# Gated scan: near levels as compact strips of 32 keys, far levels as exact products, factor products on one engine

## Chip, cores and metric

The kernel runs on one core of a Trainium2 chip. The time is that of the device for one execution, in microseconds, as the median of three runs. The core has TensorE (matrix products, into PSUM), VectorE, ScalarE and GpSimd (elementwise work), SyncE (here the weight DMAs) and 16 DMA engines. Each engine runs a program of its own, and they meet at semaphores.

## What is computed

The reference is two transformer-like blocks on 512 tokens of width 1024. The part that matters here is the first block's gated scan, once forward and once backward, for 4 heads with 128 key channels:

```python
def step(state, inp):
    qc, kc, vc, gc = inp
    bcum = jnp.cumsum(gc, axis=1)
    total = bcum[:, -1]
    new_state = jnp.exp(total)[..., None] * state + jnp.einsum(
        'bshk,bshv->bhkv', kc * jnp.exp(total[:, None] - bcum), vc)
    decay = jnp.exp(jnp.where(causal, bcum[:, :, None] - bcum[:, None], -jnp.inf))
    scores = jnp.einsum('bthk,btshk,bshk->bhts', qc, decay, kc)
    o = jnp.einsum('bhts,bshv->bthv', scores, vc) + jnp.einsum(
        'bthk,bhkv->bthv', qc * jnp.exp(bcum), state)
    return new_state, o

o_lf, _ = chunk_gated_scan(ql, klf, il, llf, s_cf, True)
o_lb, _ = chunk_gated_scan(flip(ql), flip(klb), flip(il), flip(llb), s_cb, True)
hg = hgrn2_readout(o_lf + flip(o_lb), p[..., O_HG:O_FN], hg_norm_g[l])
```

The score of query t and key s carries, for each channel, the product of all gates between them. Queries later than the key belong to the forward scan, earlier ones to the backward scan.

## The kernel before

Everything is fp32 with channels on the 128 partitions and tokens along the free axis. The scan works on blocks of 128 tokens (`TT` = 4 blocks of the 512 tokens, `TAT` = 6 with the context). `hq` holds the queries (one 512-column row for each of `HH` = 4 heads), `kk` the keys of both directions (d = 0 forward, 1 backward; 768 columns a head, context included), `ff` the gates, `q_dec` the queries with factors, kept in `hT`.

Instead of a cumulated exponent the kernel builds the products of gates by doubling. Level `lev` of `LEVELS` = 7 deals with the pairs of key and query that lie in the two halves of one group of 2 x 2^lev tokens. A unit is one level of one head: `lev_units` has 28, level by level with the four heads inside, unit u writing PSUM bank u % 4. For each unit:

- TensorE (L1143, L1144) multiplies, for each block of 128 tokens, all 128 keys of the block with the 64 queries of the later halves (forward), then with the 64 queries of the earlier halves (backward). So 8 products, most of whose entries belong to no pair of this level.
- VectorE multiplies the queries of the halves by the factors (L1099, L1101), picks the entries of this level out of the bank into the score matrix `wsc` with the constant mask `cross{lev}` (L1103), and halves the table of factors of the unit before (`shrink`, L1081).
- GpSimd multiplies the keys of the halves by the factors (L1066, L1068).

The entries of a token with itself come first: TensorE multiplies the sum of both directions' keys with the queries, 4 products a head (L1127), and ScalarE copies the bank to `wsc` (L1116), which shares the memory of `hq` and so waits for the products of the queries with the gates (L1073 on VectorE, L1055 on GpSimd).

Between the units TensorE's program computes modulation vectors: 64 `mod_step`s (L456), each a 128x32 stationary with 512 moving columns into one of four strips of 32 partitions, 2 or 3 after each unit, with a weight chunk of 2 MB for each eight. After each eighth, ScalarE copies the row (L466), and `mod_turn` (L472, 4 products with 2 columns) turns it. The first step of a chunk waits for the copy of the row before. The weights come through a ring of three slots by SyncE's queue. A barrier ends the block; the next one (L1207, L1231, L1216 to L1219) forms the states and the output out of `wsc`.

The order within each engine is the order in which the program is written. TensorE's unit u waits for the queries, the keys and the selection of unit u - 4, the same head's unit of the level before; VectorE's and GpSimd's units wait for TensorE's unit (`lev_done`) and for the factors of u - 4 (`t_upd`).

Of the kernel before, what the change touches and what calls it, by code (L numbers as in the profile page):

```python
# [19 lines left out]
U32 = mybir.dt.uint32  # L20
ALU = mybir.AluOpType
# [60 lines left out]
def constants():  # L82
# [18 lines left out]
    for lev in range(LEVELS):  # L101
        out[f"cross{lev}"] = level_mask(lev, True) + level_mask(lev, False)
# [91 lines left out]
def program(nc, weights, consts_d, vecs_d, x_d, ctx_d, out_d):  # L194
    ctx = ExitStack()
    with ctx:
# [29 lines left out]
        def bank(b, n=512):  # L226
            return psum[:, b * 512:b * 512 + n]
# [12 lines left out]
        ARENA = 22760  # L240
# [725 lines left out]
        o_hg = sb("o_hg", [P, 2, T], s6)  # L966
        k_sum = state.rearrange("p a b c -> p (a b c)")[:, 0:HH * T].rearrange("p (h n) -> p h n", h=HH)
# [73 lines left out]
        def products_of(ap, lev):  # L1041
# [8 lines left out]
            sem(n) for n in ("diag_done", "w_set", "qf_set", "qb_set", "lev_done", "sel_done", "q_upd", "k_upd", "t_upd"))  # L1050
        with nc.Block() as block:
            @block.gpsimd
            def _(pool):
                for h in range(HH):
                    pool.tensor_tensor(q_dec[1][:, h, :], hq[:, h, :], ff[:, 1, h, 0:T], ALU.mult).then_inc(qb_set, 1)  # L1055
                for u in range(NU):
                    lev, h = lev_units[u]
                    pool.wait_ge(lev_done, u + 1)
                    if lev >= 1:
                        pool.wait_ge(t_upd, u - 3)  # L1060
                        pool.wait_ge(k_upd, u - 3)
                    for d in range(2):
                        k1, k2 = halves(kk[:, d, h, :], lev)
                        _, _, (t1, t2) = products_of(ff[:, d, h, :], lev)
                        if d == 0:
                            pool.tensor_tensor(k1, k1, t2, ALU.mult)  # L1066
                        else:
                            pool.tensor_tensor(k2, k2, t1, ALU.mult).then_inc(k_upd, 1)  # L1068

            @block.vector  # L1070
            def _(dve):
                for h in range(HH):
                    dve.tensor_tensor(q_dec[0][:, h, :], hq[:, h, :], ff[:, 0, h, 0:T], ALU.mult).then_inc(qf_set, 1)  # L1073

# [9 lines left out]
                for u in range(NU):  # L1084
# [6 lines left out]
                    else:  # L1091
                        dve.wait_ge(t_upd, u - 3)
                        dve.wait_ge(q_upd, u - 3)
                        dve.wait_ge(sel_done, u - 3)
                    for d in range(2):
                        q1, q2 = halves(q_dec[d][:, h, :], lev)
                        _, _, (t1, t2) = products_of(ff[:, d, h, 0:T], lev)
                        if d == 0:
                            dve.tensor_tensor(q2, q2, t1, ALU.mult)  # L1099
                        else:  # L1100
                            dve.tensor_tensor(q1, q1, t2, ALU.mult).then_inc(q_upd, 1)  # L1101
                    mask = C(f"cross{lev}").bitcast(U32).rearrange("p (o n) -> p o n", o=1).to_broadcast([P, TT, P])
                    dve.copy_predicated(wsc[:, h, :].rearrange("p (i n) -> p i n", i=TT), mask,  # L1103
                                        bank(u % 4).rearrange("p (i n) -> p i n", i=TT)).then_inc(sel_done, 1)
# [5 lines left out]
            @block.scalar  # L1110
            def _(act):
                for h in range(HH):
                    act.wait_ge(diag_done, h + 1)
                    act.wait_ge(qf_set, h + 1)
                    act.wait_ge(qb_set, h + 1)
                    act.copy(wsc[:, h, :], bank(4 + h % 2)).then_inc(w_set, 1)  # L1116
                for ch in range(4, 12):
                    mod_copy(act, ch)

            @block.tensor  # L1120
            def _(pe):
                for h in range(HH):
# [1609 lines left out]
```

## Time and profile before

| | us |
|---|---|
| median of 3 runs | 2749.49 |
| lowest, highest | 2744.36, 2750.85 |
| the profiled execution | 2755.42 |
| its span | 2753.3 |
| TensorE, VectorE, ScalarE, GpSimd busy in the span | 2437.4, 1002.5, 734.5, 198.6 |
| the block with the levels | from 424.6 to 531.3 |

Busy time is the time in which at least one instruction of the engine runs. Matmuls overlap each other in the array, so the mean duration of one (some 270 ns with 64 columns) is much longer than the distance between two; the distance between starts is what counts. In the records each fp32 matmul stands as two matmuls with a weight load each. The granted clock is 1.00 for TensorE's upper level of 2.4 GHz and 0.50 for 1.2 GHz.

### The profile page before, as it was taken

What the parts mean: (1) busy time and instruction counts of PE and PEld (TensorE: products, weight loads), DVE (VectorE), ACT (ScalarE), POOL (GpSimd) and SP (SyncE); (2) the same over time, 40 slices, a digit from 0 to 9 for tenths busy, and PEclk for the clock granted to TensorE, in tenths of its full rate; (3) what the DMA queues carried; (4) which work ended last, traced back from release to release, by engine and by line L of the source; (5) the groups of instructions that cost most, each with busy time, mean ns of one, the idle gap of its engine ahead of it and who ended that gap; (6) DMA issues with size and microseconds to landing.
All of it is one profiled execution on the core that took longest, in us unless ns stands there. A gap on an engine that the chain in (4) does not pass through costs nothing. (4 is left out here: it accounts for less than half of the span.)

```text
span 2753.3 us, 32259 instructions
## 1 busy us (share of the span) xinstructions
PE 2437.4 (89%) x13690; PEld 1839.1 (67%) x13690; DVE 1002.5 (36%) x1585; ACT 734.5 (27%) x1271; POOL 198.6 (7%) x239
## 2 busy tenths in 40 slices
PE   6979999987999988996687999998986777799997
PEld 3533456775888866886665888886864555588885
DVE  2013118533333334635124333423225543343333
ACT  2122200023222222313212322322213552332331
POOL 0000006400000000012000000000022440000000
PEclk8988999888999997997558999998997998899999
DMA  6120013311223111200011222212210003122210
GB/s 281 38 90 17 21 41 131 145 46 47 105 79 122 69 70 62 92 31 2 4 62 62 92 92 92 92 64 92 92 33 1 1 1 123 61 92 94 110 72 31
DMA packets 16110, 196.33 MB, mean 71 GB/s; under 512 B 1888, under 2 KB 3040, under 8 KB 3936
## 3 DMA queue, kind: packets, MB, share of 16 engines
q1 hardware_dynamic: 15392, 190.72, 18.5%
q10 hardware_dynamic: 576, 3.56, 0.3%
q8 instruction: 109, 1.79, 0.3%
q14 instruction: 33, 0.27, 0.0%
HBM read 190.08 MB, written 2.10 MB: 70 GB/s over the span
## 5 line engine op out<-in xcount | busy, mean ns | idle before, releaser
L1503 DVE TENSOR_TENSOR wsp_mlp<-ring,wsp_mlp 128x1024 fp32r<-128x1024 f32 x128 | 156.7, 1225 | 447.8 <-ACT wsp_mlp L1474 447.8
L1474 ACT CAST wsp_mlp<-ring 128x1024 fp32r<-128x1024 f32 x128 | 133.9, 1048 | 491.4 <-PE psum L1459 489.4
L1456 PE MATMUL psum<-hs_mlp,wsp_mlp 128*128 128x512 f32 x512 | 201.7, 394 | 36.2 <-DVE wsp_mlp L1503 36.2
L1456 PE MATMUL psum<-acts_mlp,wsp_mlp 128*128 128x512 f32 x512 | 202.4, 395 | 0.0
L1458 PE MATMUL psum<-hs_mlp,wsp_mlp 128*128 128x512 f32 x512 | 201.3, 393 | 0.0
L1459 PE MATMUL psum<-hs_mlp,wsp_mlp 128*128 128x512 f32 x512 | 201.1, 393 | 0.0
L1459 PE MATMUL psum<-acts_mlp,wsp_mlp 128*128 128x512 f32 x512 | 199.3, 389 | 0.0
L1458 PE MATMUL psum<-acts_mlp,wsp_mlp 128*128 128x512 f32 x512 | 199.2, 389 | 0.0
L1503 DVE TENSOR_TENSOR wsp_ffn<-ring,wsp_ffn 128x1024 fp32r<-128x1024 f32 x66 | 80.8, 1225 | 246.2 <-ACT wsp_ffn L1474 246.2
L414 PE MATMUL psum<-hsev,wspev 128*128 128x512 f32 x672 | 156.6, 395 | 0.4 <-DVE arena_low L1647 0.3
L1456 PE MATMUL psum<-hs_ffn,wsp_ffn 128*128 128x512 f32 x352 | 138.1, 392 | 19.5 <-DVE wsp_ffn L1503 19.5
L414 PEld LDWEIGHTS psum<-hsev,wspev 128*128 128x128 f32 x672 | 127.8, 191 | 28.4 <-DVE arena_low L1647 1.6
L1474 ACT CAST wsp_ffn<-ring 128x1024 fp32r<-128x1024 f32 x66 | 69.1, 1048 | 266.2 <-PE psum L1459 265.2
L1458 PE MATMUL psum<-hs_ffn,wsp_ffn 128*128 128x512 f32 x352 | 137.7, 391 | 0.0
L1459 PE MATMUL psum<-hs_ffn,wsp_ffn 128*128 128x512 f32 x352 | 137.6, 391 | 0.0
L1456 PEld LDWEIGHTS psum<-hs_mlp,wsp_mlp 128*128 128x128 f32 x512 | 97.5, 190 | 58.3 <-DVE wsp_mlp L1503 37.9
L349 PE MATMUL psum<-hT,ring 128*128 128x512 f32 x288 | 125.3, 592 | 0.9 <-PEq L862 0.9
L1458 PEld LDWEIGHTS psum<-hs_mlp,wsp_mlp 128*128 128x128 f32 x512 | 97.4, 190 | 20.5
L1459 PEld LDWEIGHTS psum<-hs_mlp,wsp_mlp 128*128 128x128 f32 x512 | 97.4, 190 | 20.3
L1456 PEld LDWEIGHTS psum<-acts_mlp,wsp_mlp 128*128 128x128 f32 x512 | 96.1, 188 | 21.7 <-issue 1.9
L1458 PEld LDWEIGHTS psum<-acts_mlp,wsp_mlp 128*128 128x128 f32 x512 | 96.1, 188 | 21.6 <-issue 1.9
L1459 PEld LDWEIGHTS psum<-acts_mlp,wsp_mlp 128*128 128x128 f32 x512 | 96.1, 188 | 19.8
(391 smaller groups left out, 4152.9 us busy)
## 6 DMA issues: line engine op xcount, KB each, us to landing
ring<-weights SPq DMA_DIRECT2D x85, 2048.0 KB, 7.9
ring<-weights SPq DMA_DIRECT2D x3, 1024.0 KB, 5.7
cst<-consts ACTq DMA_DIRECT2D x1, 2209.0 KB, 14.3
xT<-xin SPq DMA_DIRECT2D x2, 1024.0 KB, 7.2
out<-xT SPq DMA_DIRECT2D x1, 2048.0 KB, 6.3
ring<-weights SPq DMA_DIRECT2D x1, 1280.0 KB, 5.9
mixT<-ctxin ACTq DMA_DIRECT2D x1, 1024.0 KB, 15.5
ring<-weights SPq DMA_DIRECT2D x2, 512.0 KB, 3.4
```

What stands on the lines that cost most here:

```text
L349: last = pe.matmul(out, lhs(k), rhs(k), start=(k == 0), stop=(k == n - 1))
L414: last = pe.matmul(out, wsp[:, q % 2, a, i * 512 + j * P:i * 512 + (j + 1) * P], hs[:, b, 2 * u + i, :], **ends)
L1456: pe.matmul(tile_bank(g, j), w_hi, src[:, 0, k0 + i, :], start=(first and i == 0), stop=False)
L1458: pe.matmul(tile_bank(g, j), w_hi, src[:, 1, k0 + i, :], start=False, stop=False)
L1459: last = pe.matmul(tile_bank(g, j), w_lo, src[:, 0, k0 + i, :], start=False, stop=(last_k and i == 1))
L1474: act.copy(wsp[:, q % 2, 0, :], raw_view(q)).then_inc(s["w_hi"], 1)
L1503: dve.tensor_tensor(wsp[:, q % 2, 1, :], raw_view(q), wsp[:, q % 2, 0, :].bitcast(F32), ALU.subtract).then_inc(s["w_lo"], 1)
```

## The change

Levels 0 to 4 (`NEAR`) concern only pairs within 32 tokens. For them each block of 128 keys is taken as four strips of 32: a product takes 32 keys and the 16 queries of their halves, and writes a strip of 32 partitions. The four strips lie side by side on partitions, 32 columns for each block, so a bank's first 128 columns hold a unit, and the selection (mask `pair{lev}`) goes into a compact `w_near` of 128 columns a head. Levels 5 and 6 (`far`) compute only the entries that belong to the level, each in its place of the bank; before level 5, `nearest` places `w_near` on the diagonal of the bank by products with parts of the identity. Banks 0 to 3 then hold the full score matrices, and ScalarE copies them to `wsc` at the end. The products of the keys with the factors move from GpSimd into VectorE's program (`keys`), with the starting products of the backward queries; GpSimd does nothing in this block. The seven 128-column masks are replaced by five of 32 columns.

```diff
-    for lev in range(LEVELS):
-        out[f"cross{lev}"] = level_mask(lev, True) + level_mask(lev, False)
+    for lev in range(5):
+        m = level_mask(lev, True) + level_mask(lev, False)
+        out[f"pair{lev}"] = np.concatenate([m[32 * r:32 * r + 32, 32 * r:32 * r + 32] for r in range(4)], axis=0)
...
-        ARENA = 22760
+        ARENA = 22760 + 512
...
+        w_near = sb("w_near", [P, HH, P], s6)
...
+        def keys(eng, lev, h):
+            k1, _ = halves(kk[:, 0, h, :], lev)
+            _, _, (_, t2) = products_of(ff[:, 0, h, :], lev)
+            eng.tensor_tensor(k1, k1, t2, ALU.mult)
+            _, k2 = halves(kk[:, 1, h, :], lev)
+            _, _, (t1, _) = products_of(ff[:, 1, h, :], lev)
+            eng.tensor_tensor(k2, k2, t1, ALU.mult).then_inc(k_upd, 1)
...
-            @block.gpsimd
-            def _(pool):
-                for h in range(HH):
-                    pool.tensor_tensor(q_dec[1][:, h, :], hq[:, h, :], ff[:, 1, h, 0:T], ALU.mult).then_inc(qb_set, 1)
-                for u in range(NU):
...
                 for h in range(HH):
                     dve.tensor_tensor(q_dec[0][:, h, :], hq[:, h, :], ff[:, 0, h, 0:T], ALU.mult).then_inc(qf_set, 1)
+                    dve.tensor_tensor(q_dec[1][:, h, :], hq[:, h, :], ff[:, 1, h, 0:T], ALU.mult).then_inc(qb_set, 1)
...
                         dve.wait_ge(q_upd, u - 3)
-                        dve.wait_ge(sel_done, u - 3)
...
+                        dve.wait_ge(k_upd, u - 3)
...
+                    keys(dve, lev, h)
+                    if lev < NEAR:
+                        if lev >= 1:
+                            dve.wait_ge(sel_done, u - 3)
+                        mask = C(f"pair{lev}").bitcast(U32).rearrange("p (o n) -> p o n", o=1).to_broadcast([P, TT, 32])
+                        dve.copy_predicated(w_near[:, h, :].rearrange("p (i n) -> p i n", i=TT), mask,
+                                            bank(u % 4, P).rearrange("p (i n) -> p i n", i=TT)).then_inc(sel_done, 1)
...
                     act.wait_ge(diag_done, h + 1)
-                    act.wait_ge(qf_set, h + 1)
-                    act.wait_ge(qb_set, h + 1)
-                    act.copy(wsc[:, h, :], bank(4 + h % 2)).then_inc(w_set, 1)
+                    act.copy(w_near[:, h, :], bank(4 + h % 2, P)).then_inc(w_set, 1)
                 for ch in range(4, 12):
                     mod_copy(act, ch)
+                for h in range(HH):
+                    act.wait_ge(lev_done, NU - HH + h + 1)
+                    act.copy(wsc[:, h, :], bank(h))
...
+                def near(lev, h, out):
+                    for i in range(TT):
+                        for d in (0, 1):
+                            for r in range(4):
+                                rows = slice(32 * r, 32 * r + 32)
+                                sl = slice(i * P + 32 * r, i * P + 32 * r + 32)
+                                to = halves(out[rows, 32 * i:32 * i + 32], lev)[1 - d]
+                                last = pe.matmul(to, kk[:, d, h, sl], halves(q_dec[d][:, h, sl], lev)[1 - d],
+                                                 start=True, stop=True)
+                    return last
+
+                def far(lev, h, out):
+                    half = 1 << lev
+                    for i in range(TT):
+                        for r in range(P // half):
+                            d = r % 2
+                            to = half * (r + 1 - 2 * d)
+                            last = pe.matmul(out[half * r:half * r + half, i * P + to:i * P + to + half],
+                                             kk[:, d, h, i * P + half * r:i * P + half * r + half],
+                                             q_dec[d][:, h, i * P + to:i * P + to + half], start=True, stop=True)
+                    return last
+
+                def nearest(h, out):
+                    for i in range(TT):
+                        for r in range(4):
+                            pe.matmul(out[32 * r:32 * r + 32, i * P + 32 * r:i * P + 32 * r + 32],
+                                      ident[:, 32 * r:32 * r + 32], w_near[:, h, 32 * i:32 * i + 32],
+                                      start=True, stop=True)
...
                     for i in range(TT):
-                        last = pe.matmul(bank(4 + h % 2)[:, i * P:(i + 1) * P], k_sum[:, h, i * P:(i + 1) * P],
-                                         hq[:, h, i * P:(i + 1) * P], start=True, stop=True)
+                        for r in range(4):
+                            sl = slice(i * P + 32 * r, i * P + 32 * r + 32)
+                            last = pe.matmul(bank(4 + h % 2)[32 * r:32 * r + 32, 32 * i:32 * i + 32], k_sum[:, h, sl],
+                                             hq[:, h, sl], start=True, stop=True)
...
-                        pe.wait_ge(sel_done, u - 3)
-                    for i in range(TT):
-                        sl = slice(i * P, (i + 1) * P)
-                        out1, out2 = halves(bank(u % 4)[:, sl], lev)
-                        pe.matmul(out2, kk[:, 0, h, sl], halves(q_dec[0][:, h, sl], lev)[1], start=True, stop=True)
-                        last = pe.matmul(out1, kk[:, 1, h, sl], halves(q_dec[1][:, h, sl], lev)[0], start=True,
-                                         stop=True)
+                        pe.wait_ge(sel_done, min(u - 3, near_units))
+                    if lev == NEAR:
+                        nearest(h, bank(h))
+                    last = (near if lev < NEAR else far)(lev, h, bank(u % 4))
```

## Rows read from the trace of the kernel before

**Rows 1.** The page: busy us and share by engine; packets and MB by DMA queue.
```profile
PE 2437.4 (89%) x13690; PEld 1839.1 (67%) x13690; DVE 1002.5 (36%) x1585; ACT 734.5 (27%) x1271; POOL 198.6 (7%) x239
...
q8 instruction: 109, 1.79, 0.3%
```

**Rows 2.** Windows: stretch, length, busy of PE, PEld, DVE, ACT, POOL; clock, DMA share, GB/s.
```profile
424.50:531.30 106.80, 101.09 (x672) 68.50 (x672) 83.81 (x118) 7.02 (x12) 73.08 (x60) 1.00 0.42 158
20.00:30.00 10.00, 8.29 (x60) 4.61 (x58) 8.15 (x9) 3.31 (x5) 0.00 (x0) 1.00 1.01 430
1288.00:1347.00 59.00, 30.88 (x2060) 28.87 (x2061) 14.18 (x18) 4.68 (x8) 7.67 (x7) 0.50 0.02 4
2068.00:2080.00 12.00, 12.00 (x113) 12.00 (x111) 8.14 (x21) 1.26 (x3) 0.00 (x0) 0.51 0.00 0
```

**Rows 3.** TensorE's timeline in the levels' block: start, us, line, tiles, [idle before].
```profile
424.59 2.02 PE L1127 MATMUL psum<-arena 128*128 128x128 f32 x16 [2.78 <-PEq L969]
...
429.83 0.34 PE L1143 MATMUL psum<-hT,arena 128*128 128x64 f32 x2
...
432.64 0.44 PE L1143 MATMUL psum<-hT,arena 128*128 128x64 f32 x2
...
434.57 1.05 PE L456 MATMUL psum<-ring,arena 128*32 128x512 f32 x4
435.56 0.44 PE L1143 MATMUL psum<-hT,arena 128*128 128x64 f32 x2
435.83 0.39 PE L1144 MATMUL psum<-hT,arena 128*128 128x64 f32 x2
436.06 0.38 PE L1143 MATMUL psum<-hT,arena 128*128 128x64 f32 x2
...
529.56 1.05 PE L472 MATMUL psum<-cst,arena 128*128 128x2 f32 x8 [0.70 <-ACT arena L466]
```

**Rows 4.** Groups by form, 405 to 560 us: count, busy us, mean ns, idle before.
```profile
L1143 PE MATMUL psum<-hT,arena 128*128 128x64 f32 x224 | 44.5, 280 | 0.0
...
L1099 DVE TENSOR_TENSOR hT<-hT,arena 128x256 f32<-128x256 f32 x28 | 18.4, 655 | 22.2 <-PE psum L1144 22.1
...
L1073 DVE TENSOR_TENSOR hT<-arena 128x512 f32<-128x512 f32 x4 | 6.8, 1763 | 0.3 <-PEq L969 0.3
```

**Rows 5.** TensorE's timeline elsewhere: matmuls with small tiles, back to back.
```profile
1303.22 1.93 PE L2024 MATMUL psum<-ring 32*32 32x32 f32 x128 [1.40 <-issue]
...
2063.29 0.46 PE L349 MATMUL psum<-arena,ring 128*64 128x62 f32 x8
2063.68 1.17 PE L349 MATMUL psum<-ring,arena 128*31 128x64 f32 x64
```

**Rows 6.** VectorE's timeline in one unit of level 4.
```profile
500.03 0.42 DVE L1099 TENSOR_TENSOR hT<-hT,arena 128x256 f32<-128x256 f32 x1 [2.59 <-PE psum L1144]
500.37 1.10 DVE L1101 TENSOR_TENSOR hT<-hT,arena 128x256 f32<-128x256 f32 x1
501.39 0.72 DVE L1103 COPY_PREDICATED arena<-cst,psum 128x512 f32<-128x512 uint32 x1
502.01 0.29 DVE L1081 TENSOR_TENSOR arena<-arena 128x48 f32<-128x48 f32 x1
```

**Rows 7.** 1288 to 1347 us: the instruction queue's packets; TensorE's waits there.
```profile
q8 instruction: 16, 0.26, 2.0%
```
```profile
PE psum L2024 <- issue: 25.5, 14, 2.1
```

**Rows 8.** ScalarE's timeline: its last row copy in the block.
```profile
528.92 0.58 ACT L466 COPY arena<-psum 128x512 f32<-128x512 f32 x1 [11.91 <-PE psum L456]
```

**Rows 9.** TensorE's timeline in the opening: `mod` steps and a turn.
```profile
26.02 1.92 PE L456 MATMUL psum<-ring,arena 128*32 128x512 f32 x16
...
32.09 3.64 PE L456 MATMUL psum<-ring,arena 128*32 128x512 f32 x16 [2.39 <-DMA ring<-weights]
36.44 1.87 PE L472 MATMUL psum<-cst,arena 128*128 128x2 f32 x8 [0.71 <-ACT arena L466]
```

More of the change, by code:

```diff
@@ L1050, in program @@
             sem(n) for n in ("diag_done", "w_set", "qf_set", "qb_set", "lev_done", "sel_done", "q_upd", "k_upd", "t_upd"))
-        with nc.Block() as block:
-            @block.gpsimd
-            def _(pool):
-                for h in range(HH):
-                    pool.tensor_tensor(q_dec[1][:, h, :], hq[:, h, :], ff[:, 1, h, 0:T], ALU.mult).then_inc(qb_set, 1)
-                for u in range(NU):
[L1057 to L1068, printed above, removed]
+        NEAR = 5
+        near_units = NEAR * HH
+        def keys(eng, lev, h):
[5 more added lines that the diff above has]
+            eng.tensor_tensor(k2, k2, t1, ALU.mult).then_inc(k_upd, 1)
+        with nc.Block() as block:
             @block.vector
@@ L1093, in _ @@
                         dve.wait_ge(q_upd, u - 3)
-                        dve.wait_ge(sel_done, u - 3)
[L1095 to L1104, printed above, removed]
+                        dve.wait_ge(k_upd, u - 3)
+                    _, q2 = halves(q_dec[0][:, h, :], lev)
+                    _, _, (t1, _) = products_of(ff[:, 0, h, 0:T], lev)
+                    dve.tensor_tensor(q2, q2, t1, ALU.mult)
+                    q1, _ = halves(q_dec[1][:, h, :], lev)
+                    _, _, (_, t2) = products_of(ff[:, 1, h, 0:T], lev)
+                    dve.tensor_tensor(q1, q1, t2, ALU.mult).then_inc(q_upd, 1)
+                    keys(dve, lev, h)
[5 more added lines that the diff above has]
+                                            bank(u % 4, P).rearrange("p (i n) -> p i n", i=TT)).then_inc(sel_done, 1)
                     if u >= 1:
```

## Prediction

> **What bounds the kernel now.** I read the page first. TensorE is busy for 89% of the span, VectorE for 36%, GpSimd for 7% [rows 1]. The change touches one stage, so its wait decides, not these shares. That stage is the block of the scan's levels, from 424.5 us to 531.3 us. In the table of stretches TensorE is busy for 101.1 of its 106.8 us, all at a granted clock of 1.00, while the weight DMAs take a share of 0.42 of the engines [rows 2]. The timeline of TensorE gives the beat [rows 3]. A level unit's matmuls (L1143, L1144) run from 432.64 to 434.57 us, 1.93 us. Then 2 or 3 `mod` steps (L456) run, 0.98 us until the next unit's first matmul. The first unit starts at 429.83, 5.24 us after the block's first matmul at 424.59. The 28 units end with the last `mod_turn`, which starts at 529.56 and lasts 1.05, so at 530.6: 100.8 us for 28 units. 28 x 2.92 is 81.8, and the other 19.0 us are the eight `mod_turn`s (L472, 0.98 each), units whose `mod` steps are cut in two by such a turn, and waits of 0.78 us for ScalarE's copy of the row.
>
> The groups by form say what a unit costs [rows 4]. The level's matmuls are 128x128 stationary with 64 moving columns, L1143 with 224 records for 28 x 4 in the source and L1144 the same: each fp32 matmul is two records, so a unit is 16 pairs of weight load and matmul. Two such pairs take 0.22 us [rows 3], 0.112 us a pair. In the same stretch VectorE is busy for 83.8 us and GpSimd for 73.1 [rows 2]. VectorE waited 22.1 us for the level's matmuls (before L1099). So TensorE leads and VectorE is close behind.
>
> **The change part by part.**
> *Near levels on TensorE.* 20 of the 28 units (levels 0 to 4) go from 8 matmuls to 32, each with a 128x32 stationary, 16 moving columns and an output strip of 32 partitions, the four strips in turn. That is 64 pairs for 16. The nearest row is L349's at 2063.68 us [rows 5]: 64 pairs of 128x31 stationary with 64 moving columns over four output strips, first start to last end 1.17 us. Less one matmul's 0.22 us, that is 0.95/63 = 15 ns a pair, against 112 ns now. The 32x32 matmuls of L2024 do 128 in 1.93 us: (1.93 - 0.24)/127 = 13.3 ns. I take 15 ns, as L349's tile has the same number of rows and strips: 64 x 15 = 0.96 us a unit, and 0.14 us between it and the `mod` steps as now (432.64 + 16 x 0.112 = 434.43, and the next step starts at 434.57). The bounds are 13.3 ns and, if 16 strided columns cost what a quarter of the present pair costs, 28 ns.
>
> A rule of the Trainium skill speaks against this. TensorE: Matmul & The Clock Gate, section Back-to-back issue gap, says that start to start never falls below about 25 ns for small moving operands. L349's 15 ns and L2024's 13.3 ns are under it, so the trace does not agree where column or row strips alternate; it shows no 16-column case. By the rule's 25 ns the saving would be 1536 x 10 ns, some 15 us smaller.
>
> *Far levels.* Level 5 has 16 placements of `w_near` (`nearest`, 32 pairs) and 16 matmuls (32 pairs), 64 pairs in all, 0.96 us a unit. Level 6 has 8 matmuls of 64 columns, 16 pairs; the 128x64 row of L349 gives (0.46 - 0.23)/7 = 33 ns, 0.53 us a unit [rows 5].
>
> *Sum on TensorE.* 24 x (0.96 + 0.14 + 0.98) + 4 x (0.53 + 0.14 + 0.98) = 49.9 + 6.6 = 56.5 us, plus the 19.0 us of turns, cuts and waits, which are untouched: 75.5 against 100.8, a gain of 25.3 us.
>
> *The start of the block.* Now the products of q with the factors (four at L1073 on VectorE, four at L1055 on GpSimd) run side by side, VectorE's in 1.76 us each [rows 4]; ScalarE's copies wait for them, and TensorE's third and fourth head wait for the copies. After, VectorE does all eight; a 128x256 product alone starts the next 0.34 us after it [rows 6], and the 128x512 predicated copy the next 0.62 (501.39 to 502.01): 0.28 us for 256 columns more, so a 128x512 product takes some 0.62. The first pair is there at 424.58 + 1.3, and the copies wait for nothing but `diag_done`. `k_sum` becomes 32 pairs a head, 0.48 us; the fourth head waits for copy and matmul of the second and ends about 2.1 us in. The first unit then starts at about 426.7 in place of 429.83: 3.1 us gained (bounds 2 and 4).
>
> *VectorE.* GpSimd's work moves in front of each shrink. Alone, a 128x256 product is followed by the next after 0.34 us (500.03 to 500.37), while its follower, of the same form but with GpSimd at work, takes 1.10 [rows 6]. The keys' 128x384 products have no unshared row; they lie between 0.34 and 0.62, and I take 0.48. The predicated copy falls from 0.62 for 512 columns to 128, some 0.2. A near unit is 2 x 0.34 + 2 x 0.48 + 0.2 = 1.84 us plus its shrink (0.9 at level 0 by the same slope, 0.48, 0.3 and less after). Over the stage: 8 x 0.62 + 28 x 1.64 + 20 x 0.2 + about 8.5 = 63 us against TensorE's 78 from the same instant. At level 0 it is 2.72 against TensorE's 2.08 plus its share of turns (0.68), level for level a draw, with four heads' slack. The three waits of each VectorE unit stay; the one on `k_upd` is for its own work, done three units before, and what is queued behind it is ready. So this move costs nothing while TensorE leads. If VectorE's 128x384 products took 0.7 and the others 0.41, it would be 28 x 0.58 = 16 us more, 79: still a tie.
>
> *Instruction supply.* This is what is late next. The page counts 13,690 pairs and 109 instruction packets of 1.79 MB on queue 8 [rows 1]: 16.4 KB for about 251 instructions of TensorE. In the stretch 1288 to 1347, where L2024's pairs follow each other, 16 packets serve 2048 pairs in 59 us, one for 3.7 us, and every burst of 128 pairs (1.93 us) is followed by an idle time of 1.4 to 2.0 us that ends with "issue", 25.5 us in 14 times [rows 7]. A block of 256 instructions thus can't be run in less than 3.7 us. A near unit will hold 128 + 9 (`mod` steps) + 5 (turns) = 142 instructions, so a block is 1.8 units, 3.74 us without a turn and 4.8 with its mean share. They match by a hair. The DMA engines are at a share of 0.42 here and at 0.02 there, and a weight packet ahead of the fetch may lengthen it. Bounds: 0, and 11 blocks x 1 us = 11 us; I take 2 us, as half of the blocks have a turn in them.
>
> *End of the block.* ScalarE now copies four whole banks to `wsc` after the last row copy. Its 128x512 copies take 0.58 [rows 8]; the last starts at 528.92 and ends 529.50, and four more end near 531.8, behind VectorE's last work: 0.8 us lost (bounds 0.3 and 1.3).
>
> *Constants.* 896 columns of masks become 160: 736 x 4 bytes x 128 partitions, 377 KB less in the DMA of the constants that the opening issues. At 430 GB/s [rows 2] that is 0.9 us of a stretch in which the DMA engines are at 1.01 and TensorE waits 2.39 us for a weight chunk [rows 2, 9]. Bounds 0 and 0.9 gained; I take 0.5.
>
> **The sum.** -25.3 - 3.1 + 2.0 + 0.8 - 0.5 = -26.1 us. The profiled execution took 2755.4 (span 2753.3), 5.9 above the median of 2749.49; the three runs themselves spread over 6.5. The change is in one stage, so it counts from either: 2729.3 for an execution like the profiled one, 2723.4 for the median.
>
> **The rivals.**
> (a) *Pairs are slower or fetches later than taken.* 1536 pairs stand in levels 0 to 5. At 28 ns instead of 15 that is 20 us more and leaves a gain of 6, 2743.4. All fetch bounds used, 9 us more, give 2732. For it: no row shows 16 strided columns into a strip, nor fetches under weight traffic. Against: two rows of small tiles at 15 and 13.3 ns. With half of each, 2735 to 2740. The Trainium skill's 25 ns (TensorE: Matmul & The Clock Gate, Back-to-back issue gap) would make it 15.4 us more, 2738.8.
> (b) *The clock falls* (the other side). The granted clock is 0.50 all through the bursts of L2024, and is 0.51 in 2068 to 2080, where TensorE is busy throughout on 31-column matmuls [rows 2]: busy time alone doesn't hold the upper level. For 1.00: the `mod` steps of 512 columns remain, now in 0.98 of each 2.08 us instead of 2.92. At half clock (1.2 GHz) the 16 records of a `mod` chunk take 3.64 us instead of 1.92, and a turn 1.87 instead of 1.05 [rows 9]. A unit's `mod` part becomes 0.98 + 0.86 = 1.84: 28 x 0.87 + 8 cut ones x 0.87 + 8 turns x 0.82 = 38 us, near pairs unchanged (L2024's 13.3 ns is at 0.50), fetch stalls gone: -26 + 36 = +10, 2759.5. It decides at 26/38, when over two thirds of the stage run at the lower level.
> (c) *VectorE becomes the bound*: TensorE idle before the near matmuls on `q_upd` or `k_upd`. From its 63 us it would need over 15 more; then some 2726 to 2735.
> (d) *More than expected*: neighbours of one tile shape need no pause between `mod` steps and near matmuls (0.12 + 0.14 now, up to 28 x 0.25 = 7 us) and pairs at 13.3 ns (2.6 us): 2714.
>
> **How the numbers follow.** Forecast with its own terms' bounds (2714 to 2732): 0.60. (a) with (c) beyond 2732 but clearly faster: 0.15. The end of (a), or the clock low for part of the stage, within the bound of 0.3% or 8.2 us (about what a measurement of this kernel tells from no change): 0.11. (b) whole, or another loss beyond it: 0.12. Under 2714: 0.02. The range runs from 2712 to 2744, leaving out (b) and half of the cases of no change, not quite 2 in 10. Faster 0.77, same 0.11, slower 0.12.
>
> **What would show it.** Near matmuls at 64 records in about 1.2 us with 0.98 for `mod` steps between; the first at 2.1 us after the block's first matmul; the block ending near 505; VectorE's 128x256 products all near 0.42 and its waits on TensorE still there; clock 1.00 throughout; L1143's place taken by idle on "issue" of a few us at most. Wrong: a clock of 0.5 in the stage, "issue" gaps of 1 us within near units, TensorE waiting for VectorE at level 0, or near bursts of 1.8 us.

## The result, and the profile after

The changed kernel takes 2729.26 us (median of six runs, 2722.03 to 2738.35); the kernel before, run beside it on the same chips, takes 2745.8 us (six runs, 2744.03 to 2750.85). The ratio is 0.9938, with a 95% interval of 0.9919 to 0.9957: 17 us faster, where 26.1 were forecast. The time lies in the forecast range.

The profiled execution of after took 2728.66 us, in the middle of its runs. That of before took 2755.42, which is some 10 us over the median of its six runs. The two spans therefore differ by 26.7 us, and that agreement with the forecast of 26.1 is an accident. What the change did has to be read from its stage. Here is the page of after: busy time by engine, and the packets of the instruction queue (packets, MB, share of the DMA engines).

```profile
PE 2392.6 (88%) x14938; PEld 1803.5 (66%) x14938; DVE 985.1 (36%) x1637; ACT 735.2 (27%) x1275; POOL 125.5 (5%) x179
...
q8 instruction: 118, 1.93, 0.3%
```

TensorE's busy time has gone down although it has 1248 more pairs of weight load and matmul to run than in [rows 1], and the instruction queue fetched nine more packets of 16.4 KB. The stretches of the block come next, in the columns of [rows 2]: length; busy time of TensorE's matmuls, its weight loads, VectorE, ScalarE and GpSimd; granted clock; DMA share; GB/s. The first is the whole block, from its first matmul to the first transpose of the next stage.

```profile
421.30:510.70 89.40, 64.95 (x1921) 36.69 (x1921) 66.33 (x170) 7.71 (x16) 0.00 (x0) 0.92 0.53 192
426.80:433.60 6.80, 5.86 (x168) 3.15 (x170) 4.62 (x12) 0.00 (x0) 0.00 (x0) 0.50 0.03 6
```

The block takes 89.4 us in place of 106.8: 17.4 us less, close to the 16.5 between the medians. TensorE is busy for 64.95 us instead of 101.1 [rows 2], 36 us less, but it now stands idle for 24.5 us instead of 5.7. The second row shows that the clock, 1.00 throughout before, is at 0.50 for part of the block: three stretches, 13.6 us in all. They begin at 426.79, 454.09 and 474.57, the first and the third still within an idle time on "issue" (4.4 and 3.5 us), the second 1.1 us after one of 2.2 us. Not every such idle time has a low stretch behind it: none follows the 3.2 us before 496.60. What ended TensorE's idle times is in the view of waits (us, times, longest):

```profile
PE psum L1129 <- issue: 13.4, 5, 4.4
PE psum L1139 <- issue: 3.2, 1, 3.2
PE psum L1147 <- issue: 1.3, 2, 1.1
PE psum L1129 <- DVE hT L1096: 1.0, 2, 0.7
```

L1129 holds the near levels' matmuls, L1139 the far ones', L1147 the placements of `w_near`. Three quarters of the idle time, 17.9 us, end with "issue": TensorE waited for no other engine. VectorE held it up for 1.0 us. In the timeline of TensorE (start, us, line, operands, count, idle time before) single near units look like this:

```profile
421.31 0.75 PE L1158 MATMUL psum<-arena 128*32 128x32 f32 x64 [2.78 <-PEq L971]
422.85 0.51 PE L1129 MATMUL psum<-hT,arena 128*32 128x16 f32 x38
427.74 0.55 PE L1129 MATMUL psum<-hT,arena 128*32 128x16 f32 x25 [4.38 <-issue]
...
442.97 0.72 PE L1129 MATMUL psum<-hT,arena 128*32 128x16 f32 x63 [0.72 <-DVE hT L1096]
...
471.17 0.58 PE L1129 MATMUL psum<-hT,arena 128*32 128x16 f32 x43
475.22 0.35 PE L1129 MATMUL psum<-hT,arena 128*32 128x16 f32 x11 [3.47 <-issue]
...
496.60 0.22 PE L1139 MATMUL psum<-hT,arena 128*32 128x32 f32 x1 [3.16 <-issue]
...
510.69 0.52 PE L1235 MATMUL psum<-cst,arena 128*128 128x128 f32 x3 [1.15 <-PEq L1064]
```

An undisturbed unit (442.97) has its 63 recorded matmuls done in 0.72 us: with one matmul's 0.19 us taken off, (0.72 - 0.19)/62 = 8.5 ns a pair. In the two disturbed ones (422.85 and 471.17) the 64 matmuls are torn apart inside one unit by 4.38 and 3.47 us in which nothing was awaited.

The groups by form of TensorE's near matmuls and of one VectorE product, 405 to 560 us (columns as in [rows 4]), and four instructions out of VectorE's timeline in a unit of level 1:

```profile
L1129 PE MATMUL psum<-hT,arena 128*32 128x16 f32 x1280 | 20.5, 193 | 14.4 <-issue 13.4 <-DVE hT L1096 1.0
L1093 DVE TENSOR_TENSOR hT<-hT,arena 128x256 f32<-128x256 f32 x28 | 11.8, 422 | 21.6 <-PE psum L1129 13.8 <-PE psum L1139 7.7
...
442.74 0.55 DVE L1062 TENSOR_TENSOR arena<-arena 128x384 f32<-128x384 f32 x1
443.21 0.29 DVE L1102 COPY_PREDICATED arena<-cst,psum 128x128 f32<-128x128 uint32 x1
443.41 0.89 DVE L1077 TENSOR_TENSOR arena<-arena 128x384 f32<-128x384 f32 x1
444.20 0.44 DVE L1093 TENSOR_TENSOR hT<-hT,arena 128x256 f32<-128x256 f32 x1
```

### The profile page after: what moved, and what is told of

Read it like the earlier page. It is cut to its first block and busy times, and to the rows that moved or that the text cites. A ratio compares the mean times of both kernels' runs of the same rounds, so it can differ in the third digit from the quotient of the medians.

```text
span 2726.6 us, 34723 instructions
## 1 busy us (share of the span) xinstructions
PE 2392.6 (88%) x14938; PEld 1803.5 (66%) x14938; DVE 985.1 (36%) x1637; ACT 735.2 (27%) x1275; POOL 125.5 (5%) x179
## 3 DMA queue, kind: packets, MB, share of 16 engines
q8 instruction: 118, 1.93, 0.3%
## 5 line engine op out<-in xcount | busy, mean ns | idle before, releaser
L1502 ACT CAST wsp_ffn<-ring 128x1024 fp32r<-128x1024 f32 x66 | 69.1, 1048 | 265.2 <-PE psum L1487 264.2
## 6 DMA issues: line engine op xcount, KB each, us to landing
mixT<-ctxin ACTq DMA_DIRECT2D x1, 1024.0 KB, 15.7
```

Of the source, the lines that this page charges most:

```text
L1502: act.copy(wsp[:, q % 2, 0, :], raw_view(q)).then_inc(s["w_hi"], 1)
```

## The experiments

Two theories stood at the start. F: the block is held by the supply of TensorE's instructions, and the 2 MB weight transfers that run beside it lengthen the fetches. V: VectorE, which took over GpSimd's products, holds it, or would as soon as the fetches don't. All ratios are against the kernel before, run on the same chip.

**Take the weight traffic away.**

```diff
+THIN = {f"mod{i}" for i in range(4, 12)} | {"out0", "out1"}
-                w = PLAN[i][1]
+                w = min(64, PLAN[i][1]) if PLAN[i][0] in THIN else PLAN[i][1]
```

> The changed kernel, with ten weight chunks (mod4 to mod11, out0, out1) loading 64 of their 4096 columns a partition, so that the modulation vectors and the output projection are computed from old contents of the ring. TensorE's program is the same. Theory F (the instruction packets wait behind the weight transfers): the idle times on issue in the levels' block fall from 18 us to under 4, the block from 89 us to 72 to 77, the ratio to the kernel before from 0.994 to 0.985 to 0.989. Rival C (the gaps come from the packets' own 3.7 us, as in the 32x32 bursts, weights or not): gaps of 1 to 2 us remain in each second unit, the block stays over 83 us, ratio 0.992 or more. Rival V (VectorE is what is waited for): no change.

> Control: the kernel before with the same ten chunks loading 64 columns, so with the same parts of the computation made of old contents. Here a packet lasts for over 14 us of TensorE's work. Theory F and both rivals: ratio 0.998 to 1.000, and the levels' block stays at 106.8 us within 1.

Measured: the changed kernel with thin loads 2707.44 us, ratio 0.9848 (0.9816 to 0.9880); the kernel before with thin loads 2749.28 us, ratio 0.9996 (0.9983 to 1.001), its block 106.8 us as ever. The window, the instruction queue's packets in it and the waits of the first:

```profile
425.30:493.70 68.40, 59.33 (x1921) 35.50 (x1922) 65.11 (x170) 7.71 (x16) 0.00 (x0) 1.00 0.06 15
q8 instruction: 15, 0.25, 1.7%
PE psum L1130 <- issue: 2.9, 3, 1.4
PE psum L1140 <- issue: 0.4, 1, 0.4
```

So weight traffic costs the kernel before nothing and the changed one 21 us of its block: the idle time on "issue" falls from 17.9 to 3.3 us, the clock stays at 1.00, and the same 1921 matmuls cost 59.3 us in place of 65.0. The count of instruction packets is the same, 15. With thin loads they come 3.5 to 4.3 us apart (mean 3.9) up to the far levels. With the weights the short and long intervals take turns: 3.4 to 4.0 us after the one before, then 6.2 to 8.5; the mean of both is 5.3. Where the long intervals come from is seen in the DMA view of two neighbouring stretches of after, 467.4 to 472.7 and 472.7 to 476.3 us:

```profile
q1 hardware_dynamic: 109, 1.79, 97.1%
q14 instruction: 1, 0.01, 0.4%
...
q1 hardware_dynamic: 35, 0.31, 21.3%
q8 instruction: 1, 0.02, 1.7%
```

In the first, a weight chunk takes 97.1% of the DMA engines and no packet of q8, TensorE's instruction queue, is seen; one of another instruction queue, q14, does get through. The next of q8 comes at 472.8, and TensorE, idle from 471.75, goes on at 475.22, as the timeline above shows. The fetch's own bytes are few (15 packets are 0.25 MB): it waits while the chunk moves. It doesn't wait for the end of the chunk. In the six transfers from 436.7 to 496.2 us, each 7.1 to 8.2 us long, the packet of q8 starts 3.9 to 5.2 us after the first weight packet and 2.1 to 3.3 us before the last has landed; in the one from 480.0 to 487.1 it starts at 484.4, with 0.49 MB of the 2 MB still to come. For comparison, an estimate from the same trace: a chunk is 128 packets of 16 KB with a median of 0.61 us, so 4.9 us for each of 16 engines, if they share it evenly. A fetch that queues behind one engine's share of the chunk would fit that; the trace doesn't name the engine of a packet, so it isn't shown.

The whole time needs one more look. The changed kernel with thin loads is 25 us better by its ratio than the changed kernel, its block 21. In its profiled execution the matmuls of the stage behind the block are quicker too, with TensorE busy for 29.0 us in place of 38.4 at a clock of 0.91 in place of 0.70. So the 21 us are read from the block and not from the whole.

**Give the keys back to GpSimd.**

```diff
+            @block.gpsimd
+            def _(pool):
+                for u in range(NU):
+                    lev, h = lev_units[u]
+                    pool.wait_ge(lev_done, u + 1)
...
+                    keys(pool, lev, h)
...
-                    keys(dve, lev, h)
```

> The changed kernel with one part undone: the key products go back to GpSimd, the strips stay. Theory F: TensorE's block is bound by packets, so it hardly changes, 89 us plus 0 to 6 where VectorE's products lengthen to 1.07 us; ratio 0.994 to 0.998. Rival V (the move of the key products is what gained, by freeing VectorE from GpSimd): the gain goes, ratio 0.999 to 1.002.

Measured: 2727.19 us, ratio 0.9925 (0.9902 to 0.9947), block 89.7.

```profile
420.90:510.50 89.60, 65.42 (x1920) 36.59 (x1920) 79.09 (x114) 7.71 (x16) 63.67 (x56) 0.92 0.52 190
PE psum L1138 <- issue: 13.0, 6, 4.4
...
L1106 DVE TENSOR_TENSOR hT<-hT,arena 128x256 f32<-128x256 f32 x28 | 29.4, 1051 | 0.0
```

With GpSimd at work the second of VectorE's two 128x256 products takes 1051 ns in place of 418, the first 683 in place of 422, so that VectorE is busy for 79.1 us with fewer instructions, against 66.3 with all of them. The block's length doesn't change (89.7 and 89.4): while fetches hold it, the move of the keys neither gains nor costs. V falls for this kernel.

The same move alone, in the kernel before:

```diff
-                    pool.tensor_tensor(q_dec[1][:, h, :], hq[:, h, :], ff[:, 1, h, 0:T], ALU.mult).then_inc(qb_set, 1)
...
+                    dve.tensor_tensor(q_dec[1][:, h, :], hq[:, h, :], ff[:, 1, h, 0:T], ALU.mult).then_inc(qb_set, 1)
...
+                            dve.tensor_tensor(k1, k1, t2, ALU.mult)
...
+                            dve.tensor_tensor(k2, k2, t1, ALU.mult).then_inc(k_upd, 1)
```

> The kernel before with the other part alone: all factor products in VectorE's program, the full 128-key products kept. Theory F: VectorE's unit is 2 x 0.34 + 2 x 0.47 + 0.62 + shrink, 2.2 to 3.1 us, against TensorE's 2.9 plus turns; the start gains about a microsecond; ratio 0.998 to 1.001, TensorE's block 105 to 108 us. Rival V: the move itself gains, ratio under 0.996.

Measured: 2741.36 us, ratio 0.9976 (0.9964 to 0.9989), just under the 0.998 to 1.001 of F and not under the 0.996 of V. The rows are the block of this kernel, the stage behind it, and the same stage of the kernel before:

```profile
422.70:528.50 105.80, 101.07 (x672) 68.45 (x672) 80.12 (x178) 7.04 (x12) 0.00 (x0) 1.00 0.42 158
528.50:565.00 36.50, 29.10 (x264) 27.62 (x264) 16.20 (x48) 12.33 (x20) 0.00 (x0) 0.90 0.12 48
...
531.40:577.00 45.60, 38.53 (x264) 36.81 (x264) 16.11 (x48) 12.34 (x19) 0.00 (x0) 0.70 0.09 37
```

The block has gained 1 us (106.8 to 105.85), though its first unit starts 4.3 us in and not 5.24. In the profiled execution the 264 matmuls of the next stage took 9 us less, because the clock stayed up. In after that stage is 46.0 us again; it is some 36.5 in the profiled executions of two more kernels, the changed one with thin loads and the one whose chunks are cut by rows (below). One execution of each doesn't show whether the block decides this, so it stays open, and so does how much of the 6.6 us of this ratio the move itself has gained.

**Keep the transfers short, so that a fetch can come between.** From the seventh `mod` chunk on, each 2 MB load is cut into four parts, each issued after a unit.

```diff
+                    for part in range(4):
+                        if part or PLAN[i][0] == "mod6":
+                            sync.wait_ge(*rest(PLAN[i][0], part))
+                        cols = slice(part * w // 4, (part + 1) * w // 4)
+                        sync.dma_start(ring[:, i % RING, cols], src[:, cols]).then_inc(weight_landed[i % RING], 16)
```

> The changed kernel, all of it computed, with the chunks mod6 to out1 each loaded in four DMAs of 512 KB, of which the later ones wait for later units of the levels. Theory F: a packet then waits for at most one such part (1.3 us), gaps fall to 3 to 8 us in total, the block to 75 to 81 us, ratio 0.986 to 0.991. Rival C: no change, 0.993 to 0.995.

Measured: 2727.09 us, ratio 0.9922 (0.9898 to 0.9947), block 89.6. The second form cuts by rows, `ring[32 * part:32 * part + 32, ...]`:

> As e4_paced, but each of the four parts of a chunk is 32 partitions with whole rows of 16 KB, so that the DMA packets keep their size; in e4_paced the parts had rows of 4 KB, eleven parts gave 1584 packets in 23 us, and the transfers ran into each other. Theory F: with parts of some 1.5 us and pauses between them the packets of instructions wait for at most one part; idle on issue 4 to 9 us, block 77 to 83 us, ratio 0.986 to 0.991. If the pacing only spreads the same delay: 0.992 to 0.995.

Measured: 2731.25 us, ratio 0.9940 (0.9916 to 0.9963), block 91.95. The windows and main waits, of the first and then the second:

```profile
425.10:514.70 89.60, 70.54 (x1921) 39.36 (x1921) 66.19 (x170) 7.71 (x16) 0.00 (x0) 0.85 0.60 189
PE psum L1147 <- issue: 5.9, 4, 2.8
PE psum L1157 <- issue: 4.5, 1, 4.5
...
421.50:513.40 91.90, 67.03 (x1920) 38.13 (x1920) 66.21 (x170) 7.71 (x16) 0.00 (x0) 0.89 0.85 185
PE psum L1147 <- issue: 12.9, 6, 4.3
```

Cut by columns, the idle time on "issue" is 11.4 us in place of 17.9, but the clock is lower (0.85) and takes the gain. Cut by rows, it is 17.6 us: the same bytes keep the DMA engines busy for a share of 0.85 instead of 0.53. Pacing is no cure, and F as it was put (a short transfer lets the fetch through) missed twice. What queues the fetch isn't settled by these runs.

**Need fewer instructions.** Strips of 64 keys instead of 32, and level 5 among the near ones: a near unit is 32 pairs with a 128x64 stationary and 32 moving columns, in place of 64.

```diff
-        NEAR = 5
+        NEAR = 6
...
-                            for r in range(4):
-                                rows = slice(32 * r, 32 * r + 32)
-                                sl = slice(i * P + 32 * r, i * P + 32 * r + 32)
-                                to = halves(out[rows, 32 * i:32 * i + 32], lev)[1 - d]
+                            for r in range(2):
+                                rows = slice(64 * r, 64 * r + 64)
+                                sl = slice(i * P + 64 * r, i * P + 64 * r + 64)
+                                to = halves(out[rows, 64 * i:64 * i + 64], lev)[1 - d]
```

> The changed kernel with strips of 64 keys in place of 32 (levels 0 to 5 compact, 256 columns a bank, one far level): half the matmuls, so some 9 instruction packets in the levels' block instead of 15, while a pair with a 64-column stationary takes about 31 ns instead of 9. Theory F: fewer packets wait behind weights, idle on issue falls from 18 us to 2 to 6, the pairs cost 0.4 us more a unit; block 76 to 82 us, ratio 0.986 to 0.991. Rival P (the array's time for the pairs decides, not their supply): 24 units x 0.4 = 10 us longer than now, ratio 0.997 to 0.999.

Measured: 2717.78 us, ratio 0.9876 (0.9848 to 0.9904), block 80.3, inside the 76 to 82 expected. The window, the packets and two lines of the timeline:

```profile
422.80:503.10 80.30, 75.25 (x1153) 43.31 (x1154) 69.63 (x174) 8.14 (x16) 0.00 (x0) 1.00 0.56 211
q8 instruction: 9, 0.15, 0.7%
...
430.11 1.05 PE L457 MATMUL psum<-ring,arena 128*32 128x512 f32 x4
431.09 1.12 PE L1129 MATMUL psum<-hT,arena 128*64 128x32 f32 x32
```

A pair costs (1.12 - 0.23)/31 = 29 ns, over three times the 8.5 of the 32-key strips, and TensorE is busy for 10 us more. Yet the block is 9 us shorter than after's: nine packets suffice, no idle time ends with "issue", and the clock stays at 1.00. The same kernel with thin loads shows that nothing of the fetches' cost is left:

> Strips of 64 keys with the ten chunks loading 64 columns as in e1_thin (so modulation and output projection of old ring contents). Theory F: with 10 packets nothing was waited for in e6_s64, so the block stays at 80.3 us within 1, where strips of 32 gained 21 us from the same edit. Rival (weight traffic slows matmuls or VectorE in another way): block 70 to 76 us.

Measured: 2720.12 us, ratio 0.9913 (0.9898 to 0.9927); its block is 80.3 us again.

```profile
421.90:502.20 80.30, 75.22 (x1152) 43.27 (x1152) 69.69 (x174) 8.14 (x16) 0.00 (x0) 1.00 0.05 12
```

Its whole time is no better than that of the kernel with full loads, although less is loaded. The two were run on different chips, each against the kernel before beside it, and the rest of the program varies by about as much. The block is the sharper measure, though each block is that of one profiled execution. Pacing by rows on top of it:

> Both: strips of 64 keys and chunks paced by rows. Theory F: hardly a packet is waited for; block 74 to 78 us, ratio 0.985 to 0.989, so 1 to 4 us under e6_s64. If the strips of 64 alone leave no wait, equal to e6_s64 within 0.001.

Measured: 2722.81 us, ratio 0.9892 (0.9862 to 0.9922), block 84.7 against an expected 74 to 78: a miss. Here are its DMA share over the block and the median time of a part from issue to landing:

```profile
q1 hardware_dynamic: 1520, 16.78, 93.7%
...
ring<-weights SPq DMA_DIRECT2D x32, 512.0 KB, 9.1
```

A 512 KB part over 32 rows needs 9.1 us to land, and the DMA engines are at 93.7% for bytes that took 55.3% before. The block is 4.4 us longer than without the pacing: 1.2 are idle time on "issue", which was none before, and 3.2 are TensorE's busy time, with the clock at 0.50 for 7 us (mean 0.96).

**Fewer changes between `mod` steps and level units.** The eight steps of a chunk run together behind every third or fourth unit instead of 2 or 3 behind each.

```diff
-                    for m in range(64 * u // NU, 64 * (u + 1) // NU):
-                        ch, k = 4 + m // KD, m % KD
-                        if k == 0:
-                            view = take(pe, f"mod{ch}").rearrange("p (k n) -> p k n", k=KD)
-                        if k == 2 and ch > 4:
-                            mod_turn(pe, ch - 1)
-                        mod_step(pe, view, ch, k)
+                    if 8 * u // NU > 8 * (u - 1) // NU and u:
+                        mod_turn(pe, 4 + 8 * u // NU - 1)
+                    if 8 * (u + 1) // NU > 8 * u // NU:
+                        ch = 4 + 8 * u // NU
+                        view = take(pe, f"mod{ch}").rearrange("p (k n) -> p k n", k=KD)
+                        for k in range(KD):
+                            mod_step(pe, view, ch, k)
```

With the 64-key strips:

> Strips of 64 keys (e6_s64) with the mod steps grouped as in e10_grouped. Here packets are 10 and were not waited for, so the same 23 us come off TensorE's time, until VectorE (some 62 to 66 us in this block) or the packets (10 x 5.9) bind. Theory F: block 64 to 72 us instead of 80.3, ratio 0.981 to 0.986; TensorE waits for q_upd or k_upd, or on issue, a few us. Rival: no gain over e6_s64, 0.987 to 0.990.

With the changed kernel's strips of 32, and with the kernel before:

> The changed kernel with the mod steps in groups of eight (a whole chunk after units 3, 6, 10, 13, 17, 20, 24, 27) in place of 2 or 3 after each unit. Eight steps in four strips take 1.92 us, sections of 1 to 3 steps 0.98 each, so TensorE's own time in the block falls by 28 x 0.98 + 8 + 3 - 8 x 1.92 = about 23 us. Theory F (packets bind, 15 of them at about 5.9 us each under the weight transfers): TensorE only reaches the next packet sooner, idle on issue grows from 18 to 30 to 40 us, block 82 to 90 us, ratio 0.992 to 0.995. Rival P (TensorE's own time binds): block 66 to 72 us, ratio 0.985 to 0.988.

> The kernel before with the mod steps grouped in the same way, full products and GpSimd as before, 6 packets. TensorE's time falls from 106.8 to about 84 us, but VectorE has 83.8 us of work in this block, beside GpSimd. Theory F with VectorE next: block 88 to 96 us, ratio 0.993 to 0.997, TensorE waiting for L1101's product or the selection.

Measured, in this order: 2707.02 us, ratio 0.9866 (0.9851 to 0.9882), block 69.1; 2721.77 us, ratio 0.9910 (0.9882 to 0.9939), block 86.4; 2747.23 us, ratio 0.9998 (0.9975 to 1.0021), block 110.9.

```profile
421.60:490.70 69.10, 59.31 (x1153) 44.10 (x1153) 68.75 (x174) 8.14 (x16) 0.00 (x0) 0.89 0.67 253
PE psum L1129 <- DVE arena L1102: 5.9, 6, 1.7
PE psum L1129 <- issue: 0.6, 1, 0.6
...
422.60:509.00 86.40, 61.45 (x1921) 41.77 (x1921) 65.94 (x170) 7.72 (x16) 0.00 (x0) 0.66 0.54 197
PE psum L1129 <- issue: 15.7, 5, 4.1
...
422.00:532.90 110.90, 108.24 (x673) 86.93 (x674) 83.36 (x118) 7.04 (x12) 74.09 (x60) 0.71 0.40 152
```

The first row is the shortest block with full loads. TensorE's matmuls cost 59.3 us, 16 less than with the steps spread. It is the `mod` steps that got cheaper, as the groups by form of the grouped kernel and of the one with the steps spread show, and that with the clock lower (0.89 against 1.00):

```profile
L1129 PE MATMUL psum<-hT,arena 128*64 128x32 f32 x768 | 28.8, 233 | 6.5 <-DVE arena L1102 5.9 <-issue 0.6
L457 PE MATMUL psum<-ring,arena 128*32 128x512 f32 x128 | 17.7, 677 | 0.0
...
L457 PE MATMUL psum<-ring,arena 128*32 128x512 f32 x128 | 37.7, 604 | 3.1 <-ACT arena L467 3.1
L1129 PE MATMUL psum<-hT,arena 128*64 128x32 f32 x768 | 27.0, 224 | 0.0
```

A spread section of four records takes 1.05 us, a group of sixteen 1.92. TensorE now waits 5.9 us for VectorE's predicated copy, and VectorE is busy for 68.75 of 69.1 us: here V comes true, and the next limit is VectorE. It was expected at 64 to 72 us; the ratio came out just above the expected 0.981 to 0.986. It is the fastest kernel here that loads all its weights, 20 us under the changed one by its ratio, which is what its block gained (89.4 - 69.1).

The second row says that with strips of 32 the grouping helps little: the waits on "issue" were expected at 30 to 40 us and came to 22.7 (15.7 of them at the near levels), and the clock was down for 58 of 86.4 us. The third was expected at 88 to 96 us and missed by far. TensorE is busy for 108.2 of 110.9 us, and yet the clock falls to 0.50 in the stretches of 64-column matmuls between the groups (mean 0.71), so that several groups run at 0.50 too and take 3.64 us instead of 1.92. With the steps spread between its units, the same kernel is at 1.00 [rows 2].

## Why the prediction was right in its direction and range, and wrong in three of its terms

*The forecast by its terms, for the block.* It said 106.8 - 25.3 - 3.1 + 2.0 + 0.8 = 81.2 us; measured were 89.4. The table takes it apart; each number is worked out below.

| step | forecast, us | measured, us |
|---|---|---|
| near pairs | 15 ns each | 8.5 ns: 10 more gained |
| start of the block | -3.1 | -3.7 |
| end of the block | +0.8 | +0.4 |
| instruction supply | +2.0 (0 to 11) | +17.9 |
| clock | none | +5.6 |

Added to the forecast, that is 81.2 - 10 - 0.6 - 0.4 + 15.9 + 5.6 = 91.7, 2.3 more than measured; these 2.3 us (pauses between units, waits for ScalarE) weren't assigned.

*Pairs.* L349's 15 ns [rows 5] belong to 64 moving columns; they were taken as they are for 16. The bounds were set at 13.3 and 28, and the pair took 8.5 ns: a near unit lasts 0.55 us instead of 0.96, and 1536 x 6.5 ns = 10 us. The lower bound was L2024's 13.3 ns, and the prediction itself says that this row stands at a granted clock of 0.50 [rows 2]. The changed kernel with grouped steps has near units at both levels; here is one at 0.50, timeline and window:

```profile
457.51 1.11 PE L1129 MATMUL psum<-hT,arena 128*32 128x16 f32 x64
...
457.50:458.60 1.10, 1.10 (x69) 1.05 (x61) 0.60 (x2) 0.59 (x1) 0.00 (x0) 0.50 0.07 15
```

It lasts 1.11 us, 13 to 15 ns a pair, where the unit at 442.97 of after, at 1.00, lasts 0.72. So a price read at the lower level was taken as the lower bound for matmuls at the upper one. By the rule of the Trainium skill weighed in the prediction (TensorE: Matmul & The Clock Gate, Back-to-back issue gap), no issue comes sooner than 25 ns. The 8.5 ns of four alternating strips are a third of that, the 29 ns of two 64-key strips lie above it; the trace of after doesn't bear the rule out as a floor.

*Start and end.* The first near unit starts at 422.85, 1.54 us behind the block's first matmul; 2.1 were forecast. The block's end waits 1.15 us behind the barrier in place of 0.76. The mechanisms and sizes held.

*The `mod` sections.* They were left at 0.98 us a unit, and at a clock of 1.00 that held: with the clock up (thin loads) the 128 records of the `mod` steps cost 37.6 us of TensorE, as in the kernel before (37.7 us). In after they cost 41.5, which is 3.9 of the clock's 5.6 us below. That they could be halved by standing together was not seen in advance.

*VectorE.* The 128x256 products take 0.42 us, all of them, as forecast for the case without GpSimd. The prices of the forecast are distances from start to start, and they held: a 128x384 product of the keys is followed after 0.47 us (0.48 was taken), the predicated copy after 0.20 (0.2 was). The shrinks were priced too low: at level 1, 0.79 us (443.41 to 444.20) where 0.48 was taken. VectorE is busy for 66.3 us, forecast 63. TensorE waited for it 1.0 us. Rival (c) did not come.

*Instruction supply.* This is the step that failed. It got the mechanism. It counted 11 packets, those of the near levels; the whole block needs 15. It took 3.7 us for a block of 256 instructions from a stretch in which the DMA engines carried a share of 0.02 [rows 2, 7], said that a weight packet ahead of the fetch may lengthen it, and priced this at no more than 1 us a block. In fact the fetch came 6.2 to 8.5 us after the one before each time a weight chunk was on its way, up to 4.8 us more than 3.7, and TensorE stood still for 17.9 us. The thin loads show both halves. Without weight traffic the fetches come every 3.9 us, much as in the bare stretch, and 3.3 us are lost, about what was forecast. With it, 14.6 more. The quick pairs have a part in this: at 8.5 ns, 1.8 units without a turn last 1.8 x (0.55 + 0.14 + 0.98) = 3.0 us (an estimate), and not the 3.74 that matched 3.7 by a hair. In the kernel before the same chunks cost nothing: in its block it needs 6 packets, one for 18 us, and even 8.5 us are covered. The runs agree that it takes both, many packets and weight traffic beside them: 15 under traffic lose 17.9, 15 without lose 3.3, 9 under traffic lose none (1.2 with the chunks cut by rows).

A page of the Trainium skill bears on this: Advanced Engine Details and Errata, ISA Cache, says that a line is 16 KB and holds 256 instructions, and the trace agrees (118 packets, 1.93 MB). Another page of the Trainium skill, Runtime: NRT & Kernel Launch, Instruction fetch mechanics, says that the fetch is hidden because the engine dispatches more slowly than its memory fills. That doesn't hold here: 256 instructions in steps of 8.5 ns a pair are gone in some 1.1 us, and one packet for 3.4 us at best has come.

*The clock.* Rival (b) came in small. The clock fell only in or behind idle times that the fetches had made, for 13.6 us of the block, and TensorE's busy time is 65.0 us in place of the 59.3 with thin loads, 5.6 us. The two paced kernels run the same matmuls with the clock down for 20.5 us (cut by rows) and 27.3 us (by columns), and their busy time is 67.0 and 70.5 us: it grows by 0.4 us for each us at the lower level, whatever the weight traffic. At 1.00 throughout, with thin loads, the near units themselves don't let the clock fall; so for this kernel it is a consequence of the fetches and no second cause. Together the two, 14.6 and 5.6, are nearly all of the 21.0 us between the two blocks, 89.4 - 68.4.

*Constants.* The opening's programs are the same in nearly all these kernels, and its end varies between 420.9 and 425.4 us. The 0.5 us forecast for the constants can't be told apart in that.

*The total.* The forecast is 26.1 us and the change brought 17. The excess of the near pairs (10) and of the start and end (1) covered half of what the fetches and the clock took (21.5 against a forecast of 2). That errors of opposite sign left the time inside the range is luck, and so is it that the measured 2729.26 is the 2729.3 forecast for an execution like the profiled one: from the median the forecast was 2723.4, and the kernel before, run beside this one, had come down to 2745.8. The block's own 89.4 us against 81.2 say more on the prediction than the total does.

## What to carry to other kernels

When many small matmuls replace a few large ones, count the 16 KB instruction packets that the stage will need, and divide its forecast time by them. Here a packet came every 3.9 us with the DMA engines quiet, and every 5.3 us on average, single ones up to 8.5, with a 2 MB weight chunk after each eight steps. The best tile is then not the one whose matmuls are cheapest but the one that keeps below the fetches, and 64-key strips at 29 ns a pair beat 32-key ones at 8.5. A price taken from a quiet stretch (packets, in our case), or from one at the lower clock level (the pairs), should be carried into another only with a row that shows it there.

## What the runs showed of the hardware that was not expected

- A pair of weight load and matmul, fp32, with a 128x32 stationary and 16 moving columns over four output strips in turn, goes at 8.5 ns start to start at a granted clock of 1.00 and at 13 to 15 ns at 0.50; with 128x64, 32 columns and two strips, 29 ns at 1.00.
- TensorE's instruction fetch is held up by a 2 MB weight transfer: no packet of that queue in 467.4 to 472.7 us, at a share of 97.1% for the weights. In six transfers it came 3.9 to 5.2 us after the first weight packet and 2.1 to 3.3 us before the end of the last. Cutting the transfers in four left 11.4 us (by columns) and 17.6 us (by rows) of idle time on "issue"; by rows, a part of 512 KB took 9.1 us to land in the kernel with 64-key strips.
- In the kernel before with grouped steps, TensorE was busy for 108.2 of 110.9 us and the mean granted clock was 0.71; with the same steps spread between the same matmuls it was 1.00.
- Two or three `mod` steps between level units hold TensorE for about 1 us whether they are 4 records or 6, but 16 records in a row take 1.92 us: 128 records cost 37.7 us spread and 17.7 grouped. What the first ones wait for, the runs don't show.
- VectorE's 128x256 product of fp32 takes 0.42 us alone and, as the second of its pair, 1.05 us beside GpSimd's products.
